# One weight block of a fused two-block kernel stored in HBM as eight groups of 16 rows, so that its load is cut for eight DMA engines

## The reference, cut to what matters

```
u = jnp.take(expert_u, eidx, axis=0)
h = jax.nn.gelu(jnp.einsum('thkd,td->thk', u, xb))
vv = jnp.take(expert_v, eidx, axis=0)
return jnp.einsum('thk,thkd->td', (g * h.astype(jnp.float32)).astype(xb.dtype), vv)
```

```
kv = (mem_n @ w_mem_kv).reshape(b, m, 2, X_HEADS, X_HEAD_DIM)
mk, mv = kv[:, :, 0], kv[:, :, 1]
```

## Time and profile before

| | us |
|---|---|
| median of 3 runs | 1153.78 |
| lowest and highest | 1153.6, 1154.17 |
| span of the profiled execution, first to last instruction | 1151.8 |

### The profile page before, as it was taken

One profiled execution on the slowest core, in us unless ns is written; L12 is line 12 of the kernel. 1 busy time (PEld: TensorE's weight loads), 2 busy tenths in 40 slices (PEclk: granted clock), 3 DMA queues, 4 the chain that ended last, 5 costly groups with the idle time before them and its releaser, 6 DMA issues.

```text
span 1151.8 us, 12055 instructions
## 1 busy us (share of the span) xinstructions
PE 1048.5 (91%) x4100; PEld 669.5 (58%) x4100; DVE 770.0 (67%) x1502; ACT 567.0 (49%) x1235; POOL 290.9 (25%) x261
## 2 busy tenths in 40 slices
PE   8999998998899779799887877889999999999998
PEld 7888554454354234344332322349878778888886
DVE  5788777667666657676676665564675496777743
ACT  7664544544543444543444345354765555444432
POOL 0001545544544334454443444400000000000000
PEclk9999999999999999999999999999999999999999
DMA  9848999999999999999999999977433454555540
GB/s 346 346 161 306 420 422 422 421 421 422 421 420 422 420 422 421 411 421 423 422 419 422 423 420 422 422 307 270 181 147 135 157 189 159 183 188 193 195 156 36
DMA packets 55532, 371.87 MB, mean 323 GB/s; under 512 B 6192, under 2 KB 7344, under 8 KB 12080
## 3 DMA queue, kind: packets, MB, share of 16 engines
q0 software_dynamic: 36864, 268.45, 56.1%
q1 hardware_dynamic: 18608, 102.65, 24.1%
HBM read 370.03 MB, written 1.05 MB: 322 GB/s over the span
## 4 chain that ended last, share of the span: by engine, by line
PE 57%; DMA 28%; DVE 6%; ACT 5%; issue 2%; POOL 1%; DVEq 0%; POOLq 0%; ACTq 0%
DMA uv<-in_peer_uv,eidx 28%; PE bank L2284 15%; PE bank L1970 8%; PE bank L1972 8%; PE bank L1971 8%; PE bank L2460 6%; PE bank L2042 4%; PE bank L2459 3%; DVE uv L1579 2%; DVE w_lo L1288 1%; PE bank L1941 1%; ACT diag L1026 1%; POOL uv L730 1%; ACT chosen L1023 1%; PE bank L2160 1%
## 5 line engine op out<-in xcount | busy, mean ns | idle before, releaser
L2284 PE MATMUL bank<-uv,diag 128*128 128x512 f32 x1024 | 486.9, 610 | 89.6 <-ACT diag L1026 89.3
L1579 DVE SCALAR_TENSOR_TENSOR uv<-uv,xn 128x1024 f32<-128x1024 f32 x256 | 313.8, 1226 | 211.7 <-DMA uv<-in_peer_uv,eidx 211.6
L730 POOL DMA_INDIRECT uv<-in_peer_uv,eidx x256 | 290.6, 1135 | 456.3 <-PE bank L2284 329.2
L2284 PEld LDWEIGHTS bank<-uv,diag 128*128 128x128 f32 x1024 | 183.9, 192 | 355.5 <-issue 353.4
L1288 DVE TENSOR_TENSOR w_lo<-wraw,w_hi 128x2048 fp32r<-128x2048 f32 x69 | 157.7, 2290 | 92.2 <-ACT w_hi L806 92.1
L1018 ACT ACTIVATE chosen<-chosen 128x1 f32<-128x1 f32 x256 | 51.8, 202 | 331.7 <-DVE uv L1579 331.3
L806 ACT CAST w_hi<-wraw 128x2048 fp32r<-128x2048 f32 x69 | 131.6, 1908 | 123.6 <-PE bank L2460 62.0
L2460 PE MATMUL bank<-nT_both,w_hi 128*128 128x512 f32 x320 | 109.6, 396 | 0.0
L1026 ACT ACTIVATE diag<-const,chosen 128x128 f32<-128x128 f32 x256 | 102.8, 401 | 8.3
L1023 ACT ACTIVATE chosen<-chosen 128x1 f32<-128x1 f32 x256 | 75.3, 294 | 9.3
L2459 PE MATMUL bank<-nT_both,w_lo 128*128 128x256 f32 x280 | 78.1, 279 | 0.0
(11 more groups left out here) (331 smaller groups left out, 1371.0 us busy)
## 6 DMA issues: line engine op xcount, KB each, us to landing
wraw<-in_ff_in SPq DMA_DIRECT2D x22, 1024.0 KB, 4.7
wraw<-in_ff_out SPq DMA_DIRECT2D x11, 1024.0 KB, 4.7
wraw<-in_query SPq DMA_DIRECT2D x4, 1024.0 KB, 5.1
uv<-in_peer_uv,eidx POOLq DMA_INDIRECT x256, 15.0
wraw<-in_in_q SPq DMA_DIRECT2D x2, 1024.0 KB, 7.8
wraw<-in_in_k SPq DMA_DIRECT2D x2, 1024.0 KB, 8.3
wraw<-in_pool_o SPq DMA_DIRECT2D x2, 1024.0 KB, 4.6
wraw<-in_sb_o SPq DMA_DIRECT2D x2, 1024.0 KB, 4.7
```

The costliest lines, as they stand in the source:

```text
L730: pool.indirect_dma_start(out=uv[:, RING_AT[n % RING], :], out_offset=None, in_=io["peer_uv"], in_offset=bass.IndirectOffsetOnAxis(ap=eidx ...
L1579: nc.vector.scalar_tensor_tensor(out=u, in0=u, scalar=1.0, in1=xn[:, head // PEER_HEADS, :], op0=ALU.mult, op1=ALU.mult, accum_out=hdot[he ...
L2284: mm = nc.tensor.matmul(acc[m][:, :], diag[:, n % RING, :], uv[:, RING_AT[n % RING], D + m * HALF:D + (m + 1) * HALF], start=False, stop=( ...
```

## The change

The block `mem_k` is stored in HBM as 8 groups of 16 rows of 2048 floats, with one further row of zeros behind each group (8 x 17 rows, not 128). The load reads the first 16 rows of each group. The source of the transfer is thereby an access pattern of three dimensions, 8 x 16 x 2048, whose slowest is 8 and can't be merged with the next because of the gaps; it was 128 x 2048. The destination, 128 partitions of one `wraw` slot, and the values in it are the same. No instruction is added, removed or moved on any engine, and no wait or semaphore changes. All other blocks, `mem_v` too, are loaded as before.

```
+GROUPS = 8
...
-                sp.dma_start(wraw[:, b % R_SLOTS, :], io[name]).then_inc(w_loaded[b % R_SLOTS], 16)
+                w = io[name]
+                if name == "mem_k":
+                    w = w[:, 0:P // GROUPS, :]
+                sp.dma_start(wraw[:, b % R_SLOTS, :], w).then_inc(w_loaded[b % R_SLOTS], 16)
...
     blocks(a["w_mem_kv_2"], ["mem_k", "mem_v"], S)
+    w = io["mem_k"].reshape(GROUPS, P // GROUPS, WB)
+    io["mem_k"] = np.concatenate([w, np.zeros_like(w[:, 0:1])], 1)
```

## The result

| | before | after |
|---|---|---|
| median of 4 runs each | 1153.69 us | 1165.18 us |
| lowest and highest | 1153.25, 1154.17 | 1165.11, 1165.4 |
| span of the profiled execution | 1151.8 us | 1163.4 us |

The ratio is 1.0096, with a 95% interval of 1.0085 to 1.0108. The kernel is 11.5 us slower. The forecast was 1156.3 us and its range ended at 1157.6. The sign was right; the loss was more than four times the forecast one (11.5 us, not 2.5).

What follows compares the result with a forecast made beforehand. The row stage was taken as bound by the DMA engine that ends last. Its further 64 KiB added 2.49 us to 1153.78, giving 1156.3 us; own range 1155.6 to 1157.0, full range 1151.1 to 1157.6.

Steps and rivals of the forecast that it cites:

- The sign: Whole kernel: forecast slower by 2.49 us; chances 0.40 slower, 0.15 faster, 0.45 within 0.2%.
- What bounds the kernel: Row stage: no DMA engine rests, and a gather landing later by x makes the end later by x.
- The unit: DMA: a 1 MiB block takes 2.49 us over 16 engines, 4.98 over eight, at 26.3 GB/s each.
- the rows pay L's share in full: Gathers beside mem_k's load: rows lose the last engine's 64 KiB, 2.48 us, once; the ring hides none.
- L among the eight: mem_k's load: the always-last engine is one of the eight that carry it; chance 0.58.
- Relief: Rival, mem_k's load: the last engine carries nothing; 0 to -2.49 us, 1151.3 after leading engines wait and level; chance 0.30.
- After, L among the eight: Gathers beside mem_k's load: the last engine moves 128 KiB, rows lose 4.98 us, not 2.49; +2.49 us.
- SP's issue: Issue of mem_k's load on SP: one to three times 0.33 us, next issue 43 us later; cost nothing.
- The rivals: Alternatives to +2.49 us: relief 0.30, nothing visible (1153.8) 0.06, loss with the second price 0.06.
- The landing: mem_k's load: lands in 16 to 20 us, not 10.3, with 100 us of cover; cost nothing.
- The ring: Eight gather slots: the last engine always has several rows queued; cost nothing for it, leading engines lose only slack.
- The second price: Rival, PE during mem_k's load: a 7 us gap may dip the clock, adding up to 3 us, 1159.3; chance 0.06.

Runs made afterwards that it cites:

- twice: Against before: mem_k loaded in its plain form, then once more when the first load had landed; 1156.48 us against 1154.22, ratio 1.0019.
- alone: Against before: six feed-forward blocks in various cuts, each loaded with nothing else in flight on the queue, mem_k plain; 1155.38 us against 1154.03.
- four: Against before: mem_k stored as four groups of 32 rows, loaded on four engines; 1177.73 us against 1154.03.
- own_half: Against before: mem_k's partitions 0 to 63 in two grouped loads of 32 on eight engines, 64 to 127 in one plain load; 1159.72 us against 1154.22.
- two: Against before: mem_k stored as two groups of 64 rows, loaded on two engines; 1177.98 us against 1154.23.

## Why the prediction was wrong, step by step

- *What bounds the kernel*: right. What the gathers lost came out at the end, 11.2 us of 11.5, and the second block only shifted.
- *The unit, and the rows pay L's share in full*: right. twice gave 2.49 for 64 KiB more. For one engine, alone has 512 KiB in 22.48 - 2.36 us with two groups, 26.1 GB/s. That the last engine is always the same was read from two fetches only, which is thin; the later steps of before bear it out (3.41 to 3.46 at five fetches of queue 14 between 397 and 692 us), and other fetches of that queue cost nothing, which fits if they fall on other engines.
- *L among the eight*: right, but by a guess, as the prediction says itself ("the rows hardly choose"); its chance of 0.58 was the author's estimate. No row of before shows that the load would run on eight engines, on which the forecast's +2.49 us stands, and no run numbers them; the result has 136 packets in queue 1, which is eight. The fetch costs the same step in after (3.45 us), and four puts L among the four that it uses. Relief, at 0.30, didn't occur. The sign doesn't even hang on it: with 8.9 us of slower transfers the kernel would have been some 6 us slower with L spared too (an estimate, 8.9 - 2.5). So the right sign says little for the mechanism. Relief's levelling of the engines "about 100 us later" leaned on the window 410 to 435 us, which is 30 to 55 us later and has a share of 1.01.
- *After, L among the eight: "L moves 128 KiB: the rows lose 4.98 us in place of 2.49."* **This is the step that failed.** The bytes are right. The step took 26.3 GB/s as a property of an engine. The runs showed that it depends on the cut: 220 to 247 GB/s for all 16 engines while this load was in flight, and a loss of 13.64 us where the step has 4.98. The missing term is 8.9 us of slower transfers, of the gathers as much as of `mem_k`; the prediction put it at nothing without a reason.
- *The bounds of that step*: it had none. SP's issue, which the trace doesn't show either, was bounded from both sides; here the rows of before show no transfer that is cut in another way than over all 128 partitions. The rate should have been listed as unknown. The rivals varied only which engine carries how much, never how fast.
- *The landing, 16 to 20 us*: too short, for the same reason. The slow stretch lasts until 391 us, some 23 us after the issue. That it costs nothing was right: the products of `mem_k` wait for nothing.
- *SP's issue, one to three times 0.33 us, free*: right, 0.72 us.
- *The ring costs nothing for L*: right. Gathers took up to 28.9 us to land; the share stayed at 0.99 to 1.05 during the load and fell to 0.98 for a moment behind it, in the slack of the leading engines. Only with four and two engines did it fall far enough to cost time (0.94, 0.89).
- *The second price, PE's gap and clock*: PE had nothing to do from 378 to 384 us and the granted clock fell to 0.79 and 0.71, deeper than the dip of before. It cost nothing, as taken: the first step behind the load is 2.30 us, shorter than a quiet one, so the rows waited for gathers and not for PE.

## What to carry to other kernels

Before a transfer is cut in another way than over all 128 partitions, ask whether the engines keep their rate in that cut, and not only how many run and how many bytes each has; two cuts with equal bytes on equal engines took 7.65 and 11.51 us. Where other transfers run beside it, a bad cut slows them too (here from 421 to 220 GB/s for all together), so a load with a hundred us of slack can still set the end. A DMA share of 1.0 says that the engines are busy and not that they move their full rate: read the GB/s beside it (1.01 came with 421 and with 220).

## What the runs showed of the hardware

- The rate of all 16 engines fell from 421 to 220 GB/s while eight of them carried a grouped block of 1 MiB, with a share of 1.01. The other eight were slowed too: at 26.3 GB/s each they alone would have moved 210 GB/s of gathers, and the gathers of all 16 moved 184. What holds them up, and in which part of the path, no run shows; this stays open.
- Sixteen engines with equal bytes are not enough for the full rate: 16 groups of 8 took 7.75 us alone, the plain form 4.85, and beside the gathers the rate fell to 244 GB/s.
- With a plain load of partitions 64 to 127 beside the gathers (and two quarters in front of it) the rate fell to 244 GB/s; with one of all 128 it was no less than 414.
- Rows with a gap of 8 KB between them, loaded as 128 rows on all 16 engines (rowgap, 144 packets), cost nothing (422 GB/s).
- An issue of a pattern of three dimensions took SP 0.57 to 0.81 us, a plain one of 128 partitions 0.33, the plain one of 64 partitions in own_half 0.55.
- The engine that ends last, L, is, as read from these steps, among the four that four groups use and not among the two that two groups use, if the two lie within the four. The small fetch costs the rows 0.93 to 0.96 us in before, after and four, and 0.05 in two.
